# Sample retention in a decoder step: eight batch rows one at a time, or two at a time on 128 partitions

## The chip, the cores and the metric

The kernel is one program on one core of a Trainium2 chip. The metric is the device time of one launch in microseconds (us). The profile is of one execution of the program; it names the engines PE (TensorE), DVE (VectorE), ACT (ScalarE), POOL (GpSimd) and SP (the queue that issues the weight loads).

## The reference

The program is one layer of a hybrid decoder for 256 prompt tokens and 64 sample tokens (8 batch rows of 8 steps), all in float32. One input projection feeds three branches (window attention, retention, gated MLP), which are gated, summed and projected; then a mixture of 32 experts follows. The change is in the retention branch of the sample tokens, where every batch row has a state `S` of its own (8 heads, 64 x 128):

```python
def retention(q, k, v, s0):
    ...
    def step(S, xs):
        qc, kc, vc = xs
        a = jnp.einsum('bihd,bjhd->bhij', qc, kc) * intra
        o = jnp.einsum('bhij,bjhe->bihe', a, vc) + jnp.einsum('bihd,bhde->bihe', qc, S) * q_decay[None, :, :, None]
        S = S * c_decay[None, :, None, None] + jnp.einsum('bjhd,bjhe->bhde', kc * k_decay[None, :, :, None], vc)
        return S, o
...
    ob, s_new = retention(rq, rk, rv, s0)
    ob = head_norm(ob, ret_norm_g).astype(x.dtype) * jax.nn.silu(rg)
...
    x = x + g1 * ((ga * oa + gb * ob + gc * oc) @ w_out)
```

For the sample group a chunk is the 8 steps, so `step` runs once per batch row. Both `o` (8 tokens per batch row) and the new `S` (an output, 256 KB per batch row) are needed.

## The kernel before

There are five instruction streams, written by hand, that meet at semaphores. The order on each engine is the order of the code; nothing is scheduled by a planner.

**Weights.** SP streams units of 2 MB into three slots of `ring`; a slot is loaded again when PE has consumed its unit. The input projection has 19 units. A unit is three *pieces*, one for each token tile (128, 128 and 64 tokens), and `project(n)` on PE computes the next n pieces wherever it stands in the code: the small matmuls of the branches stand between pieces. The last units are RG0, RG1 (retention gate, SiLU) and GB0, GB1 (the branch's sigmoid gate); `project` of tiles 0 and 1 is line 1264 and of tile 2 line 1271. Two further units are the output projection. Slots 3 to 5 of `ring` hold branch data (`XQK`, `XV`, `XC`, `XG`) until the branches are merged, and then expert weights. ACT empties each piece from PSUM (`take_pieces`, line 548).

**Small results** go through three PSUM banks in turn, in the order of the list `AUX`. PE waits with `aux_free(name)` until the result three places before has been taken; whoever takes a result signals `used(name)`.

**Sample retention, before.** The scores within the chunk (`ra2`) and their product with V (`ro2`, kept with features on partitions in `ro_s`) are done for all 64 sample tokens together. Then the loop `for b in range(BATCH_S)` runs on PE, DVE, POOL and ACT alike, one batch row at a time, on 64 partitions:

- PE: the state's part of the output (`ri{b}`, line 1458), the update of the state in two halves (`rs2{b}{h}`, line 1467), then `SAMPLE_PIECES[b]` pieces of projection.
- DVE: adds `ri{b}` to `ro_s` (line 1001); adds each half of the update to the state and multiplies by the decay (lines 1007, 1010), into `V[0:64, 2]`. That buffer has one copy, so from the second batch row on DVE first waits until the row before has been stored (`state_stored`).
- POOL: loads the state of row b (two buffers, `V[0:64, b % 2]`), masks the keys to the batch row (`kd`, line 453), stores the state of the row before (line 456), and in between scales the SiLU gate (line 463) and adds the bias of GB0 and GB1 (line 417).

Between the rows DVE also runs `head_norm(t)` and `merge_gmlp(t)` for tiles 0 and 1; `head_norm` hands its squares to ACT (`square_heads`, line 655) and waits for them. After the loop PE turns `ro_s` back to tokens on partitions (`rback0`, `rback1`), DVE merges tiles 0 and 1 (`merge_retention`, lines 1024 and 1025), and then does `head_norm(2)` and the merge of tile 2.

**Behind it.** PE transposes the merged tiles (line 1200), spreads the gates `g1` (line 1223), runs the output projection, and the residual, router and expert loop follow. ACT may overwrite `V` with `g1` only when all states are stored. POOL loads and splits the experts' biases (lines 490 to 498) once all three tiles are merged.

## Time and profile before

| | us |
|---|---|
| median of 3 runs | 1681.4 |
| lowest and highest of the 3 | 1680.76 and 1681.45 |
| the profiled execution, from its first to its last instruction (span) | 1684.8 |
| of it: up to the first instruction of sample retention by batch row | 496.9 |
| the loop over batch rows, from there to the first transposes of merged tiles | 96.5 |
| from there to the first matmul of the expert loop | 93.0 |
| expert loop to the end | 998.4 |

The page gives the span as the time of the profiled execution and nothing around it. TensorE is busy in 94% of it, VectorE in 29%, ScalarE in 19%, GpSimd in 6%. The stretches are read off the starts of PE's instructions in the timeline (496.86, 593.44 and 686.42 us).

### The profile page before, as it was taken

Reading aid. Unit: us, or ns where it says so; the run is one execution under the profiler, and the core shown is the slowest. Engines: PE = TensorE matmul, PEld = TensorE weight load, DVE = VectorE, ACT = ScalarE, POOL = GpSimd, SP = SyncE. Lnnn points to the kernel's source line nnn. Section 1 sums busy time; section 2 is a strip of 40 time slices with the busy share of each in tenths; the row PEclk is TensorE's granted clock in tenths of the full one; section 3 lists DMA queues with packets and bytes.
Section 4 is the critical chain, followed back from the end, with each engine's and each line's share of the span. In section 5 each row is a group of like instructions: output and inputs, shape, how many; then the busy total and the mean of one; then the engine's idle time right before and its main releaser. Section 6 shows DMA issues by size and latency. Waiting matters only on the chain.

```text
span 1684.8 us, 20411 instructions
## 1 busy us (share of the span) xinstructions
PE 1590.9 (94%) x8125; PEld 696.9 (41%) x8126; DVE 489.1 (29%) x824; ACT 317.7 (19%) x582; POOL 105.6 (6%) x107
## 2 busy tenths in 40 slices
PE   4989898979999888899999999999999999999996
PEld 4455555444565656233333333333333333333332
DVE  2141222266024645322222222222122222222224
ACT  1123332112121133111111111111111111111120
POOL 0000000112113433000000000000000000000000
PEclk8989999989999888999999999999999999999999
DMA  9462532233223363599999999999593999999993
GB/s 361 170 253 100 204 146 85 103 110 106 94 85 131 103 218 113 221 418 429 429 428 428 429 428 429 429 429 428 244 419 155 417 424 429 428 429 429 428 428 140
DMA packets 38583, 491.89 MB, mean 292 GB/s; under 512 B 4784, under 2 KB 4912, under 8 KB 9744
## 3 DMA queue, kind: packets, MB, share of 16 engines
q1 hardware_dynamic: 34144, 477.27, 68.5%
q0 software_dynamic: 4400, 14.06, 2.9%
q8 instruction: 29, 0.48, 0.1%
q14 instruction: 10, 0.08, 0.0%
HBM read 486.99 MB, written 4.33 MB: 292 GB/s over the span
## 4 chain that ended last, share of the span: by engine, by line
PE 88%; DVE 4%; DMA 4%; ACT 2%; POOL 1%; issue 1%; SPq 0%; DVEq 0%; POOLq 0%
PE ps L1592 28%; PE ps L1264 17%; PE ps L1621 14%; PE ps L1555 6%; PE ps L1541 6%; PE ps L1200 4%; PE ps L1271 4%; DMA ring<-in_w_dense 2%; PE ps L1216 1%; PE ps L1223 1%; PE ps L1597 1%; DMA out_sample_retention<-V 1%; PE ps L1322 1%; PE ps L1342 1%; PE ps L1467 1%
## 5 line engine op out<-in xcount | busy, mean ns | idle before, releaser
L1592 PE MATMUL ps<-ring,arena 128*64 128x512 f32 x2176 | 480.2, 594 | 2.8 <-issue 2.8
L1264 PE MATMUL ps<-ring,xT 128*128 128x512 f32 x672 | 313.0, 624 | 2.9 <-DMA ring<-in_w_dense 2.1
L1592 PEld LDWEIGHTS ps<-ring,arena 128*64 128x64 f32 x2176 | 156.5, 137 | 308.3 <-issue 305.7
L1621 PE MATMUL ps<-ring,arena 128*64 128x512 f32 x1088 | 248.5, 599 | 0.0
L1264 PEld LDWEIGHTS ps<-ring,xT 128*128 128x128 f32 x672 | 131.4, 200 | 165.1 <-issue 160.8
L1178 DVE TENSOR_TENSOR U<-ps,U 128x1024 f32<-128x1024 f32 (+1 forms) x102 | 124.4, 1219 | 248.8 <-PE ps L1555 248.8
L1621 PEld LDWEIGHTS ps<-ring,arena 128*64 128x64 f32 x1088 | 72.0, 137 | 168.1 <-issue 142.3
L1555 PE MATMUL ps<-arena 64*128 64x512 f32 x420 | 119.6, 636 | 0.8 <-ACT arena L734 0.8
L1541 PE MATMUL ps<-T,arena 128*64 128x512 f32 (+1 forms) x420 | 104.4, 616 | 1.2 <-DVE arena L1068 1.2
L1169 DVE TENSOR_SCALAR arena<-ps 128x512 f32<-128x512 f32 x34 | 23.5, 692 | 217.4 <-PE ps L1597 217.4
L707 ACT ACTIVATE W<-ps 128x512 f32<-128x512 f32 x35 | 21.0, 599 | 338.5 <-PE ps L1541 338.5
L1167 DVE TENSOR_SCALAR arena<-ps 128x512 f32<-128x512 f32 x34 | 23.5, 691 | 188.0 <-PE ps L1597 188.0
L1271 PE MATMUL ps<-ring,xT 128*64 128x256 f32 x672 | 77.5, 384 | 0.0
L725 ACT ACTIVATE arena<-arena 128x512 f32<-128x512 f32 x34 | 21.4, 629 | 204.5 <-DVE arena L1167 204.5
L548 ACT ACTIVATE ring<-ps 128x512 f32<-128x512 f32 (+1 forms) x48 | 23.4, 488 | 191.4 <-PE ps L1264 159.4
L1271 PEld LDWEIGHTS ps<-ring,xT 128*64 128x64 f32 x672 | 46.6, 138 | 29.7 <-issue 7.9
L1541 PEld LDWEIGHTS ps<-T,arena 128*64 128x64 f32 (+1 forms) x420 | 24.2, 136 | 76.6 <-issue 76.6
L1200 PEld LDWEIGHTS ps<-consts,arena 128*128 128x128 f32 (+3 forms) x329 | 36.1, 138 | 42.3 <-issue 40.9
L731 ACT ACTIVATE arena<-ps 128x320 f32<-128x320 f32 x34 | 14.9, 437 | 203.3 <-PE ps L1555 203.3
L1200 PE MATMUL ps<-consts,arena 128*128 128x128 f32 (+3 forms) x329 | 50.0, 280 | 0.5 <-ACT arena L622 0.5
L1216 PE MATMUL ps<-ring 128*32 128x128 f32 x768 | 32.5, 342 | 18.1 <-DMA ring<-in_w_dense 18.1
L1555 PEld LDWEIGHTS ps<-arena 64*128 64x128 f32 x420 | 33.6, 190 | 29.6 <-issue 29.6
(258 smaller groups left out, 1122.9 us busy)
## 6 DMA issues: line engine op xcount, KB each, us to landing
ring<-in_w_moe SPq DMA_DIRECT2D x192, 2048.0 KB, 14.8
ring<-in_w_dense SPq DMA_DIRECT2D x33, 2048.0 KB, 8.8
V<-in_state POOLq DMA_DIRECT2D x8, 256.0 KB, 5.7
out_sample_retention<-V POOLq DMA_DIRECT2D x8, 256.0 KB, 3.1
R<-in_x_prompt SPq DMA_DIRECT2D x1, 1024.0 KB, 16.6
arena<-in_cache_kT POOLq DMA_DIRECT2D x8, 128.0 KB, 3.7
arena<-in_cache_v POOLq DMA_DIRECT2D x8, 128.0 KB, 3.7
arena<-in_b_gate POOLq DMA_DIRECT2D x4, 256.0 KB, 4.0
```

Source lines behind the costliest of these rows:

```text
L548: A(buf[0:ROWS[t], t, c0 + c:c0 + c + w], src, func).then_inc(z_used, 1)
L1167: X.tensor_scalar(g_cut, ps[:, 0, :], LIMIT, None, ALU.min).then_inc(g_cut_ready, 1)
L1169: X.tensor_scalar(u_cut, ps[:, 1, :], LIMIT, -LIMIT, ALU.min, ALU.max).then_inc(dve_step, 1)
L1178: X.tensor_tensor(both, ps[0:r, 6:8, :], both, ALU.add).then_inc(added, 1)
L1200: return nc.tensor.transpose(out, in_, ident[0:r, 0:r], **kw)
L1216: last = mm(aux_bank(name)[32 * j:32 * j + 32, 0:128], silu_c[:, k, :], wv[:, k, 128 * j:128 * j + 128], start=(k == 0), stop=(k == KD - 1 ...
L1264: last = mm(banks[t][0], xT[:, k, t * P:t * P + P], wv[:, k, :], start=(k == 0), stop=(k == KD - 1))
L1271: last = mm(banks[2 + a][0], xT[:, k, 2 * P:TOKENS], wv[:, k, 256 * a:256 * a + 256], start=(k == 0), stop=(k == KD - 1), skip_group_check ...
L1541: last = mm(ps[64 * a:64 * a + 64, 3, :], pick[0:r, t, :], T[0:r, t, HALF * a:HALF * a + HALF], start=(t == 0), stop=(t == 2), skip_group_ ...
L1555: last = mm(ps[:, first + a, :], gateT[64 * a:64 * a + 64, t * P:(t + 1) * P], y_blk[64 * a:64 * a + 64, :], start=True, stop=True)
L1592: last = mm(ps[64 * a:64 * a + 64, half, :], xgT[:, k, j % 2, :], wv[:, k, HALF * a:HALF * a + HALF], start=(j % 2 == 0 and k == 0), stop= ...
L1621: last = mm(ps[64 * a:64 * a + 64, 2, :], actT[:, k, j - 4, :], wv[:, k, HALF * a:HALF * a + HALF], start=(j == 4 and k == 0), stop=(j == ...
```

## The change

The batch rows are taken in four pairs. A pair's two states stand on the two halves of the 128 partitions. What changes:

- All states have a place of their own (`pair_state`: three in `V`, one in `XV`), are loaded ahead and updated in place.
- The transposed queries are copied to both halves (`rqT_s`) and multiplied with a mask of 0 and 1 (`q_batch`, a new input of 128 KB, loaded with the gMLP's parameters) into `q_of`: four copies, each with the tokens of one pair only.
- The state's part of the output is summed in PSUM over the four pairs on top of the score products, with tokens on partitions (`ro2`; heads alternate between PSUM partitions 0 to 63 and 64 to 127). `ri`, `ro_s` and the turning back `rback` are gone.
- The keys are masked twice instead of eight times (`k_of`), each to two batch rows side by side, and the update is a matmul over a group of 32 tokens that gives 128 partitions: `rs2{j}{h}{row}` is pair `j + 2 * row`, half h of the heads.
- DVE's order is now `head_norm(t)`, `merge_gmlp(t)`, `update_states(t)` for t = 0 and 1, then `head_norm(2)`, `merge_gmlp(2)`, the three `silu_times` and the three merges.
- `ret_gain` and `squares` move, and SP's loads of slots 3 to 5 also wait for the stores, since one pair stands in slot 3 to 5.

```diff
-for _b in range(BATCH_S):
-    AUX += [f"ri{_b}", f"rs2{_b}0", f"rs2{_b}1"]
-AUX += ["rback0", "rback1"]
+AUX += [f"rs2{j}{h}{r}" for j in range(2) for h in range(2) for r in range(2)]
...
-    kd = cut(4096, HALF)
-    ro_s = cut(4608, HALF)
-    ret_gain = XQK[:, 0, :]
-    squares = cut(1024, D)
+    rqT_s = cut(2560, RH, 64)
+    q_of = cut(0, 4, RH, 64)
+    q_batch = cut(5632, 4, 64)
+    k_of = XQK[0:64, 0:2, :].rearrange("p j (h b d) -> p j h b d", h=RH, b=2)
+    pair_state = [V[:, 0, :], V[:, 1, :], V[:, 2, :], XV[:, 0, :]]
+    ret_gain = cut(4096, D)
+    squares = XV[:, 1, :]
...
                 sp.wait_ge(merged, 3)
+                sp.wait_ge(state_stored, 16 * BATCH_S)
...
+        pool.dma_start(q_batch.rearrange("p n q -> p (n q)"), ins["q_batch"]).then_inc(gm_in, 16)
...
-        def load_state(b):
-            pool.dma_start(V[0:64, b % 2, :].rearrange("p (h e) -> p h e", h=RH),
-                           ins["state"][b].rearrange("h d e -> d h e")).then_inc(state_in[b % 2], 16)
+        def load_states(n):
+            for b in range(2):
+                pool.dma_start(pair_state[n][64 * b:64 * b + 64].rearrange("p (h e) -> p h e", h=RH),
+                               ins["state"][2 * n + b].rearrange("h d e -> d h e")).then_inc(state_in[n], 16)
+        def store_states(n):
+            for b in range(2):
+                pool.dma_start(outs["sample_retention"][2 * n + b].rearrange("h d e -> d h e"),
+                               pair_state[n][64 * b:64 * b + 64].rearrange("p (h e) -> p h e", h=RH)).then_inc(state_stored, 16)
         pool.wait_ge(gate_bias_in, 16)
         load_gate_bias(2, 0)
         pool.wait_ge(kv_stored, 64)
-        for b in range(2):
-            load_state(b)
-        pool.wait_ge(gm_in, 64)
+        for n in range(3):
+            load_states(n)
+        pool.wait_ge(gm_in, 80)
...
-        for b in range(BATCH_S):
-            if b >= 2:
-                pool.wait_ge(new_state, 2 * (b - 1))
-                load_state(b)
-            if b == 0:
-                pool.wait_ge(roped, 3)
...
-            nc.gpsimd.tensor_scalar(kd[0:64], XQK[0:64, 2, HALF:D], const("of_batch")[0:64, b:b + 1], None, ALU.mult).then_inc(kd_ready, 1)
-            if b >= 1:
-                pool.wait_ge(new_state, 2 * b)
-                pool.dma_start(outs["sample_retention"][b - 1].rearrange("h d e -> d h e"),
...
-                pool.wait_ge(z_used, 4 * (RG1 + 1))
-                pool.wait_ge(ret_gain_in, 16)
-                for t, r in enumerate(ROWS):
...
-            if b == 5:
-                add_gate_bias(XC, 0, GB0, 4)
-                load_gate_bias(1, 1)
...
-        pool.wait_ge(new_state, 2 * BATCH_S)
...
+        load_states(3)
+        pool.wait_ge(roped, 3)
+        k3 = XQK[0:64, 2, HALF:D].rearrange("p (h d) -> p h d", h=RH).unsqueeze(2).to_broadcast([64, RH, 2, RDK])
+        for j in range(2):
+            of = const("k_batch")[0:64, 2 * j:2 * j + 2].unsqueeze(1).unsqueeze(3).to_broadcast([64, RH, 2, RDK])
+            nc.gpsimd.tensor_tensor(k_of[:, j], k3, of, ALU.mult).then_inc(k_masked, 1)
+        pool.wait_ge(z_used, 4 * (RG1 + 1))
+        pool.wait_ge(ret_gain_in, 16)
+        for t, r in enumerate(ROWS):
+            nc.gpsimd.tensor_tensor(XG[0:r, t, :], XG[0:r, t, :], ret_gain[0:r], ALU.mult).then_inc(silu_scaled, 1)
+        pool.wait_ge(new_state, 4)
+        store_states(0)
+        store_states(2)
+        add_gate_bias(XC, 0, GB0, 4)
+        load_gate_bias(1, 1)
+        pool.wait_ge(new_state, 8)
+        store_states(1)
+        store_states(3)
+        add_gate_bias(XC, 1, GB1, 5)
         pool.dma_start(outs["prompt_retention"].rearrange("h d e -> d h e"), state[0:64]).then_inc(retention_stored, 16)
...
+        aux_filled(act, "rqT2")
+        turned_q = aux_bank("rqT2")[0:64].rearrange("p (h m) -> p h m", h=8)
+        A(rqT_s[0:64], turned_q, ACT.Copy)
+        A(rqT_s[64:128], turned_q, ACT.Copy).then_inc(used("rqT2"), 1)
+        aux_filled(act, "rkT2")
...
+        gate(R, 6, 1)
         aux_filled(act, "ro2")
-        A(ro_s, aux_bank("ro2"), ACT.Copy).then_inc(used("ro2"), 1)
-        gate(R, 6, 1)
+        by_parity = U[0:64, 2, :].rearrange("p (h a e) -> p a h e", h=4, a=2)
+        A(by_parity[:, 0], aux_bank("ro2")[0:64].rearrange("p (h e) -> p h e", h=4), ACT.Copy)
+        A(by_parity[:, 1], aux_bank("ro2")[64:128].rearrange("p (h e) -> p h e", h=4), ACT.Copy).then_inc(used("ro2"), 1)
...
-        for b in range(BATCH_S):
-            take_pieces(SAMPLE_PIECES[b])
-            if b in (1, 3):
-                square_heads(b // 2)
+        for t in range(3):
+            take_pieces(2)
+            square_heads(t)
+        take_pieces(2)
         gate(XC, 12, 1)
-        for h in range(2):
-            name = f"rback{h}"
-            aux_filled(act, name)
-            A(U[0:64, 2, HALF * h:HALF * h + HALF], aux_bank(name)[0:64], ACT.Copy).then_inc(used(name), 1)
-        square_heads(2)
...
+        aux_taken(dve, "rqT2")
+        X.tensor_tensor(q_of, rqT_s.unsqueeze(1).to_broadcast([P, 4, RH, 64]),
+                        q_batch.unsqueeze(2).to_broadcast([P, 4, RH, 64]), ALU.mult).then_inc(q_masked, 1)
...
+        def update_states(j):
+            for h in range(2):
+                for row in range(2):
+                    name = f"rs2{j}{h}{row}"
+                    aux_filled(dve, name)
+                    st = pair_state[j + 2 * row][:, HALF * h:HALF * h + HALF]
+                    X.tensor_tensor(st, aux_bank(name), st, ALU.add).then_inc(used(name), 1)
+                    aux_taken(dve, name)
+                    s4 = st.rearrange("p (h e) -> p h e", h=4)
+                    done(X.tensor_tensor(s4, s4, const("chunk_decay")[:, 8 + 4 * h:12 + 4 * h].unsqueeze(2).to_broadcast([P, 4, RDV]), ALU.mult), new_state)
+        aux_taken(dve, "ro00")
+        aux_taken(dve, "ro01")
+        head_norm(0)
+        merge_gmlp(0)
+        update_states(0)
+        aux_taken(dve, "ro10")
+        aux_taken(dve, "ro11")
+        head_norm(1)
+        merge_gmlp(1)
+        update_states(1)
         aux_taken(dve, "ro2")
-        for b in range(BATCH_S):
-            if b:
-                dve.wait_ge(state_stored, 16 * b)
-            name = f"ri{b}"
-            aux_filled(dve, name)
-            mine = ro_s.rearrange("p (h t) -> p h t", h=RH)[:, :, b * STEPS:(b + 1) * STEPS]
-            X.tensor_tensor(mine, aux_bank(name)[:, 0:64].rearrange("p (h t) -> p h t", h=RH), mine, ALU.add).then_inc(used(name), 1)
-            for h in range(2):
-                name = f"rs2{b}{h}"
-                aux_filled(dve, name)
-                st = V[0:64, b % 2, HALF * h:HALF * h + HALF]
-                new = V[0:64, 2, HALF * h:HALF * h + HALF]
-                X.tensor_tensor(new, aux_bank(name)[0:64], st, ALU.add).then_inc(used(name), 1)
-                aux_taken(dve, name)
-                n4 = new.rearrange("p (h e) -> p h e", h=4)
-                done(X.tensor_tensor(n4, n4, const("chunk_decay")[0:64, 8 + 4 * h:12 + 4 * h].unsqueeze(2).to_broadcast([64, 4, RDV]), ALU.mult), new_state)
-            if b in (1, 3):
-                aux_taken(dve, f"ro{b // 2}0")
-                aux_taken(dve, f"ro{b // 2}1")
-                head_norm(b // 2)
-            if b in (0, 2, 4):
-                merge_gmlp(b // 2)
-            if b in (5, 6):
-                silu_times(b - 5)
+        head_norm(2)
+        merge_gmlp(2)
+        for t in range(3):
+            silu_times(t)
...
-        merge_retention(0)
-        merge_retention(1)
-        aux_taken(dve, "rback0")
-        aux_taken(dve, "rback1")
-        head_norm(2)
-        silu_times(2)
-        merge_retention(2)
+        for t in range(3):
+            merge_retention(t)
...
+        def sample_out(n):
+            return aux_bank("ro2")[64 * (n % 2):64 * (n % 2) + 64, n // 2 * RDV:(n // 2 + 1) * RDV]
         for n in range(RH):
-            last = mm(aux_bank("ro2")[:, n * 64:n * 64 + 64], XV[0:64, 2, n * RDV:(n + 1) * RDV], ra[0:64, 0, n * 64:n * 64 + 64], start=True, stop=True)
+            mm(sample_out(n), ra[0:64, 0, n * 64:n * 64 + 64], XV[0:64, 2, n * RDV:(n + 1) * RDV], start=(n < 2), stop=False, skip_group_check=True)
+        pe.wait_ge(q_masked, 1)
+        for i in range(4):
+            pe.wait_ge(state_in[i], 32)
+            for n in range(RH):
+                last = mm(sample_out(n), q_of[:, i, n, :], pair_state[i][:, n * RDV:(n + 1) * RDV], start=False, stop=(i == 3), skip_group_check=True)
         last.then_inc(aux_ready, 1)
-        for b in range(BATCH_S):
-            pe.wait_ge(state_in[b % 2], 16 * (b // 2 + 1))
-            name = f"ri{b}"
-            aux_free(name)
-            for n in range(RH):
-                last = mm(aux_bank(name)[:, n * STEPS:(n + 1) * STEPS], V[0:64, b % 2, n * RDV:(n + 1) * RDV],
-                          rqT[0:64, n, b * STEPS:(b + 1) * STEPS], start=True, stop=True)
-            last.then_inc(aux_ready, 1)
-            pe.wait_ge(kd_ready, b + 1)
+        project(2)
+        for j in range(2):
+            pe.wait_ge(k_masked, j + 1)
             for h in range(2):
-                name = f"rs2{b}{h}"
-                aux_free(name)
+                names = [f"rs2{j}{h}{row}" for row in range(2)]
+                for name in names:
+                    aux_free(name)
                 for n in range(4):
                     hh = 4 * h + n
-                    last = mm(aux_bank(name)[0:64, n * P:n * P + P], kd[0:64, hh * RDK:(hh + 1) * RDK],
-                              XV[0:64, 2, hh * RDV:(hh + 1) * RDV], start=True, stop=True)
-                last.then_inc(aux_ready, 1)
-            project(SAMPLE_PIECES[b])
-        aux_taken(pe, f"ri{BATCH_S - 1}")
-        for h in range(2):
-            name = f"rback{h}"
-            aux_free(name)
-            for n in range(4):
-                hh = 4 * h + n
-                last = tr(aux_bank(name)[0:64, n * P:n * P + P], ro_s[:, hh * 64:hh * 64 + 64], P)
-            last.then_inc(aux_ready, 1)
+                    for row, name in enumerate(names):
+                        last = mm(aux_bank(name)[:, n * P:n * P + P], k_of[32 * row:32 * row + 32, j, hh].rearrange("p b d -> p (b d)"),
+                                  XV[32 * row:32 * row + 32, 2, hh * RDV:(hh + 1) * RDV], start=True, stop=True)
+                last.then_inc(aux_ready, 2)
+                project(1)
...
+def query_batches():
+    own = np.arange(64)[None, None, :] // STEPS == np.arange(BATCH_S).reshape(4, 2).T[:, :, None]
+    return np.repeat(own, 64, axis=0).reshape(P, -1).astype(np.float32)
```

On PE, from the score products of the sample (`ro2`) on; line 1264 is pieces of tiles 0 and 1 (x8 for one piece), line 1271 a piece of tile 2. Before:

```order
L1450 MATMUL ps<-arena,ring 128x64 x8
L1458 MATMUL ps<-arena,V 128x8 x8
L1467 MATMUL ps<-ring,arena 64x128 x8
L1264 MATMUL ps<-ring,xT 128x512 x8
L1271 MATMUL ps<-ring,xT 64x256 x16
L1458 MATMUL ps<-arena,V 128x8 x8
L1467 MATMUL ps<-ring,arena 64x128 x8
L1264 MATMUL ps<-ring,xT 128x512 x16
```

The same place after the change:

```order
L1457 MATMUL ps<-ring,arena 64x128 x8
L1462 MATMUL ps<-V,arena 64x128 x24
L1462 MATMUL ps<-ring,arena 64x128 x8
L1264 MATMUL ps<-ring,xT 128x512 x8
L1271 MATMUL ps<-ring,xT 64x256 x16
L1475 MATMUL ps<-ring 128x128 x8
L1264 MATMUL ps<-ring,xT 128x512 x8
L1475 MATMUL ps<-ring 128x128 x8
L1264 MATMUL ps<-ring,xT 128x512 x8
L1475 MATMUL ps<-ring 128x128 x8
L1271 MATMUL ps<-ring,xT 64x256 x16
L1475 MATMUL ps<-ring 128x128 x8
```

The state's matmuls now all stand in one place (line 1462), and of the update there are four groups (line 1475), each with one piece behind it; the eight pieces that were spread over eight batch rows follow with the last two together.

On DVE, from the masking of the sample's scores (line 963) on. Before, with the first batch row and `merge_gmlp(0)`:

```order
L963 TENSOR_TENSOR arena<-ps,consts 64x512
L1001 TENSOR_TENSOR arena<-ps,arena 128x8x8
L1007 TENSOR_TENSOR V<-ps,V 64x512
L1010 TENSOR_TENSOR V<-V,consts 64x512
L1007 TENSOR_TENSOR V<-ps,V 64x512
L1010 TENSOR_TENSOR V<-V,consts 64x512
L984 TENSOR_TENSOR W<-W,R 128x1024
L985 TENSOR_TENSOR T<-T,W 128x1024
```

The same place after the change, up to the first half state:

```order
L963 TENSOR_TENSOR arena<-ps,consts 64x512
L966 TENSOR_TENSOR arena<-arena 128x2048
L973 TENSOR_REDUCE stat<-U 128x8
L974 TENSOR_SCALAR stat<-stat 128x8
L975 TENSOR_TENSOR U<-U,stat 128x1024
L977 TENSOR_REDUCE stat<-ring 128x8
L978 TENSOR_SCALAR stat<-stat 128x8
L980 RECIPROCAL stat<-stat 128x8
L981 TENSOR_TENSOR U<-U,stat 128x1024
L987 TENSOR_TENSOR W<-W,R 128x1024
L988 TENSOR_TENSOR T<-T,W 128x1024
L1004 TENSOR_TENSOR V<-ps,V 128x512
```

`head_norm(0)` (lines 973 to 981) and `merge_gmlp(0)` (987, 988) now stand ahead of the first state update (1004), which frees PE's banks.

On ACT, in the residual behind the output projection, where the sum of squares (line 694) is followed by a square root (line 515); a piece of the difference:

```order
 L548 ACTIVATE W<-ps 128x512
 L694 ACTIVATE W,stat<-R 128x1024
+L515 ACT_TABLE_LOAD
 L515 ACTIVATE stat<-stat 128x1
 L548 ACTIVATE W<-ps 128x512
```

Before, the table of the square root was still loaded from `head_norm(2)`; now the sigmoid of the gates comes last ahead of the residual, and the load of the table stands behind the first sum of squares.

## Rows read from the trace of the kernel before

**Rows 1.** The page, its first line

```profile
span 1684.8 us, 20411 instructions
```

**Rows 2.** Chain that ended last, 495 to 605 us: start, us, what

```profile
562.69 4.78 POOL ring L417 x3
...
570.93 10.51 DMA out_sample_retention<-V
```

**Rows 3.** Timeline of DVE, the mask of the sample's scores

```profile
488.14 0.68 DVE L963 TENSOR_TENSOR arena<-ps,consts 64x512 f32<-64x512 f32 x1 [3.68 <-PE ps L1444]
```

**Rows 4.** Timeline of PE: start, us, what, [idle before it]

```profile
495.02 2.00 PE L1450 MATMUL ps<-arena,ring 64*128 64x64 f32 x16
...
501.64 9.40 PE L1264 MATMUL ps<-ring,xT 128*128 128x512 f32 x16
...
516.45 1.96 PE L1467 MATMUL ps<-ring,arena 64*64 64x128 f32 x16
...
518.34 14.00 PE L1264 MATMUL ps<-ring,xT 128*128 128x512 f32 x32
...
566.76 3.67 PE L1271 MATMUL ps<-ring,xT 128*64 128x256 f32 x32
...
575.57 3.67 PE L1467 MATMUL ps<-ring,arena 64*64 64x128 f32 x16
...
593.44 1.97 PE L1200 MATMUL ps<-consts,T 128*128 128x128 f32 x8 [2.37 <-DVE T L1025]
...
603.93 1.09 PE L1223 MATMUL ps<-mod,consts 128*64 128x128 f32 x8 [2.92 <-ACT V L675]
...
604.95 15.70 PE L1264 MATMUL ps<-ring,xT 128*128 128x512 f32 x32
```

**Rows 5.** Timeline of PE, other places

```profile
172.63 1.95 PE L1216 MATMUL ps<-ring 128*32 128x128 f32 x64
...
702.44 1.13 PE L1555 MATMUL ps<-arena 64*128 64x512 f32 x4
```

**Rows 6.** Timeline of POOL and DVE, 520 to 542 us

```profile
521.45 6.94 POOL L463 TENSOR_TENSOR ring<-ring 128x1024 f32<-128x1024 f32 x3
...
521.69 6.74 DVE L971 TENSOR_SCALAR stat<-stat 128x8 f32<-128x8 f32 x1
...
537.42 0.67 DVE L1007 TENSOR_TENSOR V<-ps,V 64x512 f32<-64x512 f32 x1
...
541.54 1.23 DVE L985 TENSOR_TENSOR T<-T,W 128x1024 f32<-128x1024 f32 x1
```

**Rows 7.** Chain and timeline around the gMLP's parameters, 357 to 373 us

```profile
357.39 8.46 DMA arena<-in_mixT_s
...
372.32 3.78 PE L1390 MATMUL ps<-ring,arena 128*128 128x128 f32 x16 [8.04 <-DVE ring L930]
```

**Rows 8.** Timeline of ACT, 570 to 646 us

```profile
570.48 0.78 ACT L548 ACTIVATE ring<-ps 64x256 f32<-64x256 f32 x2 [6.78 <-PE ps L1271]
...
573.21 1.06 ACT L554 ACTIVATE ring<-ring 128x1024 f32<-128x1024 f32 x1 [0.65 <-POOL ring L417]
...
599.71 1.28 ACT L515 ACT_TABLE_LOAD   x1
...
645.91 0.20 ACT L515 ACTIVATE stat<-stat 128x1 f32<-128x1 f32 x1 [0.29 <-DVE stat L760]
```

**Rows 9.** Timeline of POOL and DVE behind the merge

```profile
607.04 0.59 POOL L479 DMA_DIRECT2D arena<-in_router_w  x1 [12.68 <-DVE T L1025]
...
640.33 2.12 POOL L497 TENSOR_TENSOR U<-U,consts 32x1024 f32<-32x1024 f32 x1
...
640.43 2.56 DVE L1049 TENSOR_TENSOR W<-W,V 128x512 f32<-128x512 f32 x1 [5.47 <-ACT W L548]
```

**Rows 10.** Stretches: busy time of each engine, then granted clock of TensorE

```profile
512.00:533.00 21.00, 21.00 (x97) 11.77 (x93) 12.14 (x8) 1.98 (x5) 10.23 (x6) 1.00 0.37 125
...
580.00:593.00 13.00, 9.03 (x40) 8.00 (x40) 9.01 (x13) 1.18 (x2) 3.48 (x5) 0.50 0.16 38
```

43 lines of the change are left out of this document (18 added, 25 removed).

## The prediction

> **What bounds the kernel now.** The page gives a span of 1684.8 us [rows 1]; the median of the runs shown is 1681.4, 3.4 less. I make the sum against the span and move the median by it. First I read the chain that ended last between 495 and 605 us. Up to about 556 us it is PE alone. Then it hops: POOL's bias of the gates, a store of 10.51 us behind it, DVE, another store and DVE's merges [rows 2]. The single new-state buffer makes each batch row wait for the store of the row before. Next I read PE's timeline there: the last input piece ends at 566.76 + 3.67 = 570.43 us, the first transposes of merged tiles start at 593.44, and PE idles or works on crumbs at the lower clock between them (granted 0.50 in 580 to 593, which is 1.2 GHz, against 1.00, 2.4 GHz, in 512 to 533) [rows 4, 10]. So 23.0 us lie between last piece and merge, of which only the gate path is needed: ACT ends the first sigmoid at 573.21 + 1.06 = 574.27 us, 3.84 behind the last piece [rows 8]. Two DVE operations of 1.23 follow [rows 6]: 6.3 us would do. All behind it is PE's, in a row, up to the expert loop, whose loads are released by PE, so an earlier start moves the end by as much.
>
> **The change, part by part**, in times of the trace before (without what is added further up, which comes last).
>
> *PE, state outputs.* PE starts the score products at 495.02 [rows 4]. Now there are 8 + 32 small matmuls, 80 rows, since the profile counts a float32 matmul twice. They have 64 output partitions in alternating halves and 128 moving columns. From below: four column groups took 1.95 for 64, so two groups 0.061 each, 4.9 us [rows 5]. From above: the update's matmuls, all on one place, took 1.96 for 16, so 9.8 us; at the lower clock 3.67 for 16, so 18 us [rows 4]. The alternation makes it nearest to the column groups: I take 5.0, and PE is at the next piece at 500.0 (before: 501.64).
>
> *PE, pieces.* A piece of tile 0 or 1 takes 7.0 (14.00 for two), one of tile 2 takes 3.6, and the one at 501.64 took 9.40, as the clock was low behind the small matmuls [rows 4]. I keep the 9.40: RG1 ends at 500.0 + 9.4 + 3.6 = 513.0. The first update group (16 rows of 32 x 128) is priced like the old one, 1.96 [rows 4]: 515.0. GB0's first piece ends at 522.0. Of update groups there are four now, 7.8 us, where there were eight.
>
> A page of the Trainium skill (TensorEngine Tiling (Array Packing), Key Properties) says that different tiles of the array work in parallel, and that changing the tiling mode drains the engine. Trace: scatter matmuls in two row halves took 1.13 for 4 of 512 columns, less than the 0.44 each of a piece [rows 4, 5]. By that rule the four groups cost 1.0 each; the two that others wait for would bring 1.9 us more, 1656.5 in the end. I keep the row of the same size.
>
> *DVE.* The query mask is 2048 elements a partition; 1024 take 1.23 [rows 6], so 2.5 us, behind the mask of the scores (488.14 + 0.68 [rows 3]): 491.3. It is hidden: PE wants it behind the score products, at about 496. Then `head_norm(0)` centres tile 0 and waits for ACT's squares, which now stand behind RG1's last piece: 513.0, a copy of 0.78, a square of 1.06 (as a sigmoid of that size) [rows 8]: 514.9. POOL starts the SiLU scaling at the same moment, and it takes 6.94; in the trace a DVE TENSOR_SCALAR of 128x8 that met it took 6.74 [rows 6]. I expect the same here, at the variance: DVE stands until 520.9. Square root, reciprocal and multiply 2.1, `merge_gmlp` 2.5: at 525.5 the first half state is added (0.7, then 0.7 for the decay [rows 6]; the same on 128 partitions as on 64), and a bank is free at 526.2. **This is the new wait**: the second update group needs that bank, and all pieces are queued behind it on PE. It idles 522.0 to 526.2.
>
> Then the group 1.95, GB0's second piece 7.0, and 2.5 for the clock behind the wait (between 15.70 against 14.00 for two pieces, and 9.40 against 7.0 for one [rows 4]): 537.7. ACT takes it, squares tile 1: 539.4. DVE finishes `head_norm(1)` (3.2) and `merge_gmlp(1)` (2.5), adds: 545.8. PE meanwhile did the third group and GB0's last piece by 543.3, and waits 2.5 for that bank. Group 1.95, piece 7.0, clock 2.5: 557.3. Two more pieces: the last ends at 568.0 (before 570.43). DVE by then: updates to 552.4, centring to 555.0, squares of tile 2 at 559.0, `head_norm(2)` 562.2, merge 564.7, three SiLU products of 1.23: 568.4. The first gate is ready at 568.0 + 3.84 = 571.8, so DVE is not late, by 3.4 us. The merge is there at 574.3 against 593.44: **-19.1**.
>
> *Stores.* Eight stores and two late loads remain, but the loads are ahead of need and nothing on DVE waits for a store. ACT's wait before `g1` is for stores issued at about 553 to 555; even one of 10.51 us [rows 2] is down by 566.
>
> *ACT behind the merge.* Before, ACT was in tile 2's head norm, and PE waited 2.92 for it at 603.93 [rows 4]. That norm is now over: **-2.9**.
>
> *Table load.* The square root in the residual now loads its table. A load takes 1.28, and before ACT idled 0.29 there for DVE [rows 8]; DVE, ACT and PE all stand on that root: **+1.0**. The Trainium skill (ScalarE: Activation LUTs, What ACT_TABLE_LOAD costs) gives 1283 ns and a drain of 1380 ns. The load's row agrees, a drain is not a row of its own. By the page it would be +2.4, 1659.8 in the end.
>
> *POOL against DVE in the residual.* At 640.43 a DVE multiply of 512 elements, elsewhere 0.67, took 2.56, beside POOL's split of the expert bias [rows 6, 9]; the add behind it was late too, 0.7. POOL's split starts when all tiles are merged (607.04 [rows 9]). That now comes at 574.3 + 5.0 = 579.3, 28 earlier, while the residual moves by 22. The split (that part 33 to 35.4 behind its start, so 612.9 to 615) is over when the residual comes at 618.4: **-2.6**.
>
> *Further up.* `q_batch` is issued ahead of the gMLP's mixing weights. Their landing (8.46 after issue) is on the chain, and PE idles 8.04 for it [rows 7]. One more issue is 0.6 [rows 9]; 128 KB more at the rate of the 1.66 MB in those 8.46 is 0.65. From below 0, from above both, 1.2, and if the four further state loads behind it shared the queue, 5 more. I take **+0.6**.
>
> Sum: -19.1 - 2.9 + 1.0 - 2.6 + 0.6 = -23.0. Span 1661.8, median **1658.4**.
>
> **The rivals.**
> *Less is lost.* POOL doesn't meet DVE, banks are free in time, and the clock stays. Then PE could be through at 556, DVE at about 564: the merge comes 7.8 earlier still, 1650.6. For it: the stretch 512 to 533 held 1.00 with the same mix [rows 10]. Against it: the 6.74 row.
> *PE's new matmuls are dear.* 9.8 to 18 us in place of 5.0; squares, banks and pieces all move with them: 1663 to 1671. For it: the clock was low just there before [rows 4].
> *The parameters come late.* The state loads share the queue: +5, 1663. Against it: they are issued behind the awaited one.
> *Slower: the clock.* If the many small matmuls and the waits keep TensorE at 1.2 GHz through the pieces (five of 7.0 and three of 3.6, 46 us), these cost 46 more, of which 7.3 are counted: 1697. It decides once more than 23 + 7 = 30 of the 46 us run low. For it: 580 to 593 at 0.50. Against it: 512 to 533 at 1.00 with PE always busy.
> *It brings nothing.* Another wait holds the merge until 593, for instance a store. Against it: no reader waits for one. 1681.
>
> **How the numbers follow.** Forecast 0.50 (its own range 1653 to 1664), less lost 0.12, dear matmuls 0.20, late parameters 0.06, slower by the clock 0.04, nothing 0.03, and 0.05 for several costs at once, beyond 1672. The range takes the first four: 1650 to 1672. A measurement here tells about 0.2% (3.4 us) from no change. Faster by more 0.93, within 0.03, slower 0.04.
>
> **What would show it.** State outputs (line 1462) in about 5 us with the mask not waited for; DVE's TENSOR_SCALAR at the first variance as long as POOL's scaling; PE idle some 4 and 2.5 us ahead of the second and fourth group (line 1475), with DVE as releaser; last piece near 568, first transposes near 574 to 575; no wait for ACT ahead of the output projection; a table load behind the first sum of squares; the residual's first multiply of the second half back at 0.7. Wrong would be: no stall at the banks, DVE behind the gate, a low clock through whole pieces, or a wait on a state load or store.

## The result and the profile after

The changed kernel takes **1661.1 us** in the median of 4 runs (1652.7 to 1667.7), beside 1681.4 us before (1680.8 to 1683.7); the ratio is 0.986, 95% interval 0.983 to 0.989. Forecast was 1658.4, with a range of 1650 to 1672. The page of the profiled execution, first line:

```profile
span 1665.9 us, 20091 instructions
```

Against [rows 1] that is 18.9 us less, in one execution of each. The four executions of the changed kernel lie 15 us apart, so a difference of two spans says little by itself. What is compared below are stretches between fixed places of the program, each measured from where PE starts the sample's score products (`ro2`). First PE in the changed kernel (columns: start, us, engine, line, operation, output<-input, count, and in brackets the idle time before it with what ended it):

```profile
500.23 1.09 PE L1457 MATMUL ps<-ring,arena 64*64 64x128 f32 x16
501.25 2.84 PE L1462 MATMUL ps<-V,arena 128*64 128x128 f32 x48
...
504.89 7.13 PE L1264 MATMUL ps<-ring,xT 128*128 128x512 f32 x16
...
515.56 1.16 PE L1475 MATMUL ps<-ring 32*128 32x128 f32 x16
...
527.70 1.27 PE L1475 MATMUL ps<-ring 32*128 32x128 f32 x16 [3.91 <-DVE V L1004]
528.90 8.67 PE L1264 MATMUL ps<-ring,xT 128*128 128x512 f32 x16
...
546.82 2.08 PE L1475 MATMUL ps<-ring 32*128 32x128 f32 x16 [4.55 <-DVE V L1004]
548.83 15.81 PE L1264 MATMUL ps<-ring,xT 128*128 128x512 f32 x32
564.57 3.67 PE L1271 MATMUL ps<-ring,xT 128*64 128x256 f32 x32
575.33 1.97 PE L1200 MATMUL ps<-consts,T 128*128 128x128 f32 x8 [7.09 <-DVE T L1030]
...
583.48 14.00 PE L1264 MATMUL ps<-ring,xT 128*128 128x512 f32 x32
...
633.70 6.87 PE L1504 MATMUL ps<-arena,xT 128*128 128x32 f32 x32
```

L1457 are the score products with the values, L1462 the state outputs (64 rows in all; the first 48 are shown), L1475 the update groups, of which the third is left out. The reader should see four things. Score products and state outputs are over 4.66 us after their start, and the piece behind them takes 7.13, not the 9.40 of [rows 4]. PE waits for DVE before the second and the fourth update group, 3.91 and 4.55 us: the new wait that was forecast. Behind each wait PE is slower for a while (8.67 for a piece of 7.13; 2.08 for a group of 1.16). And there is no wait for ACT ahead of the output projection any more (583.48), where [rows 4] had 2.92.

DVE at the first head norm and the first half state:

```profile
518.76 0.17 DVE L978 TENSOR_SCALAR stat<-stat 128x8 f32<-128x8 f32 x1
...
519.52 2.77 DVE L981 TENSOR_TENSOR U<-U,stat 128x1024 f32<-128x1024 f32 x1
522.32 3.25 DVE L987 TENSOR_TENSOR W<-W,R 128x1024 f32<-128x1024 f32 x1
...
526.86 0.69 DVE L1004 TENSOR_TENSOR V<-ps,V 128x512 f32<-128x512 f32 x1
```

and POOL, which started its SiLU scaling a microsecond before DVE went on with the head norm (517.51):

```profile
516.54 7.95 POOL L462 TENSOR_TENSOR ring<-ring,arena 128x1024 f32<-128x1024 f32 x3 [22.99 <-ACT ring L548]
```

The TENSOR_SCALAR takes 0.17 us. In [rows 6] one beside the same scaling took 6.74, and the prediction had it stand until POOL was done. What is late instead are two TENSOR_TENSOR with two inputs each, 2.77 and 3.25 in place of 1.23.

The same stretches in all profiles, in us, each worked out from the starts of PE's groups (the last piece from start plus duration):

| kernel | score products start at | to the end of the last piece | to the first transposes | to the output projection | to the expert loop | score products to expert loop, sum |
|---|---|---|---|---|---|---|
| before | 495.0 | 75.4 | 23.0 | 11.5 | 81.5 | **191.4** |
| before_again | 489.9 | 75.4 | 23.3 | 11.5 | 81.4 | 191.7 |
| after | 500.2 | 68.0 | 7.1 | 8.2 | 83.1 | **166.4** |
| after_again | 492.8 | 67.9 | 7.1 | 8.1 | 83.1 | 166.2 |
| two_buffers | 489.4 | 75.4 | 20.4 | 12.0 | 80.0 | 187.9 |
| five_slots | 490.4 | 75.4 | 14.5 | 11.5 | 85.4 | 186.8 |
| no_alternating | 490.7 | 71.1 | 7.1 | 8.2 | 83.5 | 169.8 |
| scaling_by_tile | 490.3 | 61.7 | 7.1 | 7.9 | 80.7 | 157.4 |
| banks_first | 495.2 | 55.0 | 12.1 | 8.8 | 80.5 | 156.4 |
| table_early | 485.8 | 68.1 | 7.1 | 8.2 | 80.9 | 164.3 |
| residual_clean | 490.7 | 70.3 | 7.1 | 8.5 | 80.4 | 166.2 |
| combined | 503.4 | 55.0 | 10.6 | 7.7 | 80.3 | 153.6 |

The change takes 25.0 us out of the stretch that it touches (191.4 to 166.4; 25.5 between the two repeats). Up to the router's first products (line 1504 or its like) it is 161.6 us before and 133.5 after, 28.1 less. The first column moves by 17.6 us, among kernels that are the same up to there too; that is taken up at the end.

### The profile page after: what moved, and what is told of

It is laid out like the page before. It is cut to its first block, busy times and chain, and to the rows that moved or that the text cites. A ratio compares the mean times of both kernels' runs of the same rounds, so it can differ in the third digit from the quotient of the medians.

```text
span 1665.9 us, 20091 instructions
## 1 busy us (share of the span) xinstructions
PE 1566.5 (94%) x7989; PEld 670.2 (40%) x7990; DVE 483.0 (29%) x801; ACT 318.4 (19%) x582; POOL 97.6 (6%) x102
## 4 chain that ended last, share of the span: by engine, by line
PE 89%; DVE 4%; DMA 3%; ACT 2%; issue 1%; POOL 1%; SPq 0%; DVEq 0%; POOLq 0%
PE ps L1593 28%; PE ps L1264 17%; PE ps L1622 14%; PE ps L1542 6%; PE ps L1556 6%; PE ps L1271 5%; PE ps L1200 4%; DMA ring<-in_w_dense 2%; PE ps L1223 1%; PE ps L1216 1%; PE ps L1598 1%; PE ps L1322 1%; PE ps L1342 1%; ACT ring L548 1%; PE ps L1504 1%
## 5 line engine op out<-in xcount | busy, mean ns | idle before, releaser
L1264 PE MATMUL ps<-ring,xT 128*128 128x512 f32 x672 | 309.6, 618 | 3.0 <-DMA ring<-in_w_dense 2.3
L1271 PE MATMUL ps<-ring,xT 128*64 128x256 f32 x672 | 84.1, 407 | 0.0
L1200 PEld LDWEIGHTS ps<-consts,arena 128*128 128x128 f32 (+2 forms) x321 | 35.1, 138 | 41.9 <-issue 41.6
L1200 PE MATMUL ps<-consts,arena 128*128 128x128 f32 (+2 forms) x321 | 48.5, 278 | 0.5 <-ACT arena L622 0.5
L1216 PE MATMUL ps<-ring 128*32 128x128 f32 x768 | 28.3, 311 | 18.3 <-DMA ring<-in_w_dense 18.3
## 6 DMA issues: line engine op xcount, KB each, us to landing
R<-in_x_prompt SPq DMA_DIRECT2D x1, 1024.0 KB, 16.7
```

Of the source, the lines that this page charges most:

```text
L1200: return nc.tensor.transpose(out, in_, ident[0:r, 0:r], **kw)
L1216: last = mm(aux_bank(name)[32 * j:32 * j + 32, 0:128], silu_c[:, k, :], wv[:, k, 128 * j:128 * j + 128], start=(k == 0), stop=(k == KD - 1 ...
L1264: last = mm(banks[t][0], xT[:, k, t * P:t * P + P], wv[:, k, :], start=(k == 0), stop=(k == KD - 1))
L1271: last = mm(banks[2 + a][0], xT[:, k, 2 * P:TOKENS], wv[:, k, 256 * a:256 * a + 256], start=(k == 0), stop=(k == KD - 1), skip_group_check ...
```

## The experiments

Each kernel differs from one of the two by the lines shown and the semaphores that go with them. Times are medians, ratios are to the kernel before on the same chip (its medians there were 1683.8 to 1688.1), with their 95% interval; so go by the ratios across experiments.

### The two kernels again

> The changed kernel once more, nothing edited. Theory: its first profile drew about 5 us of low clock ahead of the change (PE reached the sample's score products at 500.23 us, before 495.02), so a second profile reaches them near 495 and has a span near 1660. Rival: the 5 us belong to the change (the new load of the query mask); then they are there again. Median of the runs 1656 to 1665 either way. From the score products to the expert loop 166.4 us (first profile) by both, plus or minus 2 for the clock.

**Measured:** 1657.4 us, ratio 0.985 (0.982 to 0.988).

> The kernel before once more, nothing edited: median 1681 within 3 us. Its profile shows how far two executions of one kernel lie apart in the part ahead of the score products (495.02 us in the first): 2 to 5 us if the clock's low stretches fall by chance, under 1 if they do not.

**Measured:** 1682.4 us, ratio 1.000 (0.997 to 1.003). The stretches of the table repeat within 0.4 us, the starts of the score products don't (495.0 and 489.9; 500.2 and 492.8). A span can't be compared within 1%. A stretch can be read to some tenths only where the clock falls alike: residual_clean, which is the changed kernel up to the last piece, takes 2.3 us longer there (70.3 for 68.0). A difference of two stretches is shown below only as far as single rows account for it.

### Only the row buffers: two_buffers, five_slots

In the kernel before, a batch row's new state goes into the one buffer `V[:, 2]`, and the next row waits for its store. First with two such buffers, everything else as before:

```diff
+    new_buf = [V[:, 2, :], XV[:, 0, :]]
...
-                dve.wait_ge(state_stored, 16 * b)
+                dve.wait_ge(row_stored[b % 2], 16 * (b // 2))
...
-                new = V[0:64, 2, HALF * h:HALF * h + HALF]
+                new = new_buf[b % 2][0:64, HALF * h:HALF * h + HALF]
```

> The kernel before, with two buffers for the new state instead of one, so that no batch row waits for the store of the row before it; everything else as before. Theory A (the chain of the last rows hangs on POOL, which issues the loads of states 6 and 7 between the gate biases, as much as on the store): DVE's waits for stores go, but PE still waits for the state of row 7, issued at about 576 us, and the time falls by 1 to 3 us only. Theory B (the single buffer was the bound): the 10.3 and 2.2 us that DVE waited for stores behind the last piece come off, 10 to 13 us less, more than half of what the whole change brought.

**Measured:** 1680.6 us, ratio 0.997 (0.996 to 0.999); the stretch is 3.5 us shorter, much nearer to theory A (1 to 3) than to B (10 to 13). The chain shows why not more; where the stores stood there is a load:

```profile
569.79 4.14 DMA V<-in_state
```

In the chain this load follows directly on POOL's gate bias (567.00 to 569.50 us), behind which it stands in POOL's program; besides, it may start only when the state two rows earlier has been used up. So, later, a second form with five slots, in which no load stands behind a gate bias:

```diff
+    slots = [V[:, 0, :], V[:, 1, :], V[:, 2, :], XV[:, 0, :], XV[:, 1, :]]
...
-                st = V[0:64, b % 2, HALF * h:HALF * h + HALF]
-                new = V[0:64, 2, HALF * h:HALF * h + HALF]
+                st = new = slots[b % 5][0:64, HALF * h:HALF * h + HALF]
```

> The kernel before, with one change: each batch row's state lives in one of five slots (V tiles 0 to 2, XV tiles 0 and 1), is updated in place and stored from there, and five rows are loaded ahead; rows 5 to 7 are loaded once the store of the row five before has landed, which was issued two rows earlier. All matmuls, masks and merges of the rows stay as they are, one row after the other. It asks how much of the 25 us between score products and expert loop comes from the row buffers alone. With two new-state buffers that stretch went from 191.4 to 187.9 us, and its chain still had 4.14 us of a state load and PE waits of 0.93 and 3.81 for loads. Theory A, buffers are a part, the work of the single rows (16 groups of products instead of 8, eight query groups, the sum carried back at the end) the rest: the load waits and the low clock behind them go, about 5 to 8 us: 180 to 183 us in that stretch, ratio to before 0.993 to 0.995. Theory B, the buffers are nearly all of it: 168 to 172 us, ratio 0.987 or less. Theory C, the rows now wait on DVE in place of the loads: 186 to 188, ratio 0.997 or more.

**Measured:** 1676.0 us, ratio 0.994 (0.991 to 0.996), the ratio of theory A, but the stretch, 186.8, is as theory C had it; the ratio holds the scatter ahead of the stretch too. The table tells where the gain went: the first transposes come 8.5 us sooner than before (14.5 against 23.0 behind the last piece), and 3.9 of these are lost again behind them. PE in the residual of this kernel:

```profile
569.53 3.14 PE L1463 MATMUL ps<-arena,V 64*128 64x8 f32 x16
572.60 3.67 PE L1472 MATMUL ps<-ring,arena 64*64 64x128 f32 x16
...
640.25 1.97 PE L1205 MATMUL ps<-consts,T 128*128 128x128 f32 x8 [4.86 <-ACT W L555]
...
644.18 6.88 PE L1508 MATMUL ps<-arena,xT 128*128 128x32 f32 x32
```

There is no wait for a state at 569.53 or 572.60, but the rows still come one after another on PE behind the last piece, at the lower clock (3.14 and 3.67 us; the row before had 1.95 and 1.96). At 640.25 PE waits 4.86 us, and the router products behind it take 6.88 where the kernel before needed 3.92 and two_buffers 4.08. So a merge that comes earlier can be worth less at the end than at the merge. The slow router products are in the changed kernel too (6.87 at 633.70), but an early merge alone doesn't bring them: scaling_by_tile and residual_clean, with merges as early, take 3.80 and 3.66. Why they fall on the lower clock in some kernels stays open.

Measured from the score products to the first transposes it is 98.4 us before, 89.9 with five slots and 75.1 in the changed kernel. Of 23.3 us, buffers bring **8.5**; the other **14.8** need the rest of the change: two rows on 128 partitions, no row left behind the last piece, the sum over rows made in PSUM, DVE's new order. No run parts these from each other. At the expert loop buffers are worth 4.6 of the 25.0.

### The order of the small matmuls: no_alternating

The state outputs go into alternating halves of the output, and the update groups take alternating 32-row groups of the array. Here the same matmuls run with equal halves and equal row groups one after the other:

```diff
+        HEADS = [0, 2, 4, 6, 1, 3, 5, 7]
-        for n in range(RH):
+        for n in HEADS:
             mm(sample_out(n), ra[0:64, 0, n * 64:n * 64 + 64], ...
...
-            for n in range(RH):
+            for n in HEADS:
                 last = mm(sample_out(n), q_of[:, i, n, :], ...
...
-                for n in range(4):
-                    hh = 4 * h + n
-                    for row, name in enumerate(names):
+                for row, name in enumerate(names):
+                    for n in range(4):
+                        hh = 4 * h + n
```

> The changed kernel with the heads of the state outputs in the order 0, 2, 4, 6, 1, 3, 5, 7 (all of one half of the PSUM partitions, then the other) and the update groups with all of one 32-row group, then the other; the same matmuls, other order. Theory (neighbours on different tiles of the array run at once): the state outputs take 9.4 to 9.8 us instead of 4.7, an update group 1.96 instead of 1.09; 5 to 8 us slower in all. Rival (a matmul of that size costs that little on its own): no difference, within 2 us.

**Measured:** 1660.0 us, ratio 0.986 (0.984 to 0.987); the stretch is 3.4 us longer than in after (3.7 than in after_again), which neither side had: 5 to 8 was the theory, under 2 the rival. PE's groups changed:

```profile
490.66 1.58 PE L1458 MATMUL ps<-ring,arena 64*64 64x128 f32 x16
...
507.30 1.71 PE L1476 MATMUL ps<-ring 32*128 32x128 f32 x16
...
519.44 3.06 PE L1476 MATMUL ps<-ring 32*128 32x128 f32 x16 [3.36 <-DVE V L1004]
```

A score group takes 1.58 in place of 1.09, an update group 1.71 in place of 1.16 at the higher clock, and 3.06 behind the waits (1.27 and 2.08 there). Score products and state outputs together take 5.97 for 4.66. So the order alone is worth a third of a group; neighbours on different parts of the array overlap. The first slower group is made up by a shorter wait behind it (3.36 for 3.91). The second wait is shorter by 1.5 (3.06 for 4.55): 0.55 by the slower third group, and 0.9 because DVE's last operation of `merge_gmlp(1)` doesn't meet POOL's gate bias here (1.23 us for the 2.17 in the changed kernel). The whole medians don't show the difference: 0.986 beside 0.986 and 0.985.

### The new wait: scaling_by_tile, banks_first

Two ways to take away PE's wait for a bank. In the first, POOL scales each tile of the SiLU as soon as ACT has it, rather than all three behind the last, beside DVE's head norm:

```diff
-        pool.wait_ge(z_used, 4 * (RG1 + 1))
         pool.wait_ge(ret_gain_in, 16)
         for t, r in enumerate(ROWS):
+            pool.wait_ge(z_used, 4 * RG1 + (1, 2, 4)[t])
```

> The changed kernel, with POOL's scaling of the SiLU gate waiting for each token tile of RG1 by itself instead of all three, so that two thirds of it run while DVE is idle. Theory (POOL's reads slow DVE's multiplies at the end of head_norm(0), 2.77 and 3.25 us in place of 1.23 each): they are back at 1.23, the first wait for a bank falls from 3.9 to about 0.4 us, and the kernel gains 3 to 5 us. Rival (those two are slow for another reason, or the wait is only moved to the second bank): within 1 us.

**Measured:** 1651.6 us, ratio 0.981 (0.977 to 0.985); the stretch is 9.0 us shorter, about twice what it had been put at. By the whole times alone the gain wouldn't be shown: the interval meets those of the changed kernel's two (0.982 to 0.989). DVE and PE:

```profile
509.60 1.23 DVE L981 TENSOR_TENSOR U<-U,stat 128x1024 f32<-128x1024 f32 x1
510.86 1.23 DVE L987 TENSOR_TENSOR W<-W,R 128x1024 f32<-128x1024 f32 x1
```

```profile
514.22 1.16 PE L1475 MATMUL ps<-ring 32*128 32x128 f32 x16 [0.35 <-DVE V L1004]
515.31 7.13 PE L1264 MATMUL ps<-ring,xT 128*128 128x512 f32 x16
...
531.69 1.55 PE L1475 MATMUL ps<-ring 32*128 32x128 f32 x16 [4.55 <-DVE V L1004]
...
617.69 3.80 PE L1504 MATMUL ps<-arena,xT 128*128 128x32 f32 x32
```

DVE's two operations are back at 1.23, and the first wait is 0.35 in place of 3.91 (-3.6). The group and the piece behind the vanished wait take 1.16 and 7.13 in place of 1.27 and 8.67 (-1.7). These 5.2 us the edit brought. The groups and pieces behind the second wait take 1.1 less, and 2.4 more are saved between output projection and expert loop, where the router products take 3.80 in place of 6.87; both are clock in places that nobody edited, and no run shows that the edit brought them. The second wait, 4.55, has not moved.

In the second way DVE hands over the banks of the first half earlier, while ACT squares the tile:

```diff
+            between()                      # in head_norm, behind the centring
             dve.wait_ge(head_squared, t + 1)
...
-        head_norm(0)
+        head_norm(0, lambda: update_states(0, (0,)))
         merge_gmlp(0)
-        update_states(0)
+        update_states(0, (1,))
```

> The changed kernel with DVE's order turned around at two places: the first half of the state update (heads 0 to 3) comes directly behind the centring in head_norm(0) and head_norm(1), where DVE waits for ACT's squares anyway, instead of behind head_norm and merge_gmlp. Theory (PE's 3.91 and 4.55 us of waiting for banks, and the clock behind them, set when the last piece ends): both waits go, the last piece ends 9 to 12 us earlier, and the kernel gains 5 to 10 us, less than the piece because DVE then has to catch up at the merge. Rival (DVE's own chain is the bound, PE's wait is only its shadow): 0 to 2 us.

**Measured:** 1649.0 us, ratio 0.979 (0.977 to 0.981), the stretch 10.0 us shorter; here the interval lies clear of the changed kernel's. PE, and DVE at the first merge:

```profile
518.72 1.16 PE L1476 MATMUL ps<-ring 32*128 32x128 f32 x16
519.81 7.13 PE L1265 MATMUL ps<-ring,xT 128*128 128x512 f32 x16
...
562.35 1.97 PE L1201 MATMUL ps<-consts,T 128*128 128x128 f32 x8 [12.09 <-DVE T L1031]
```

```profile
554.16 5.62 DVE L995 TENSOR_TENSOR U<-U,ring 128x1024 f32<-128x1024 f32 x3
559.81 1.23 DVE L1030 TENSOR_TENSOR U<-U,ring 128x1024 f32<-128x1024 f32 x1
```

No group waits for a bank, no piece is slow, and the last piece ends 13.0 us sooner. But the first transposes now stand 12.1 behind it and not 7.1: DVE has no idle time ahead of its first merge (559.81 follows on 554.16 + 5.62), so of 13 us 8 arrive. DVE, not PE, sets the merge now; its three SiLU products take 5.62 in place of 3.7, beside POOL's gate bias (551.25 to 557.45).

### The residual: residual_clean, table_early

Two costs behind the merge: the square root's table, and POOL's split of the expert bias beside DVE. The first kernel takes both away:

```diff
             pool.wait_ge(b1_in, 48 * (half + 1))
+            if half:
+                pool.wait_ge(h_ready, 3)
...
         gate(XC, 12, 1)
+        A(stat[:, 94:95], stat[:, 94:95], ACT.Sqrt)
```

> The changed kernel with a square root of an unused column put behind the gates on ACT, so that its table is loaded while PE transposes, and with the second half of POOL's split of the expert bias held back until the residual is over. Theory: DVE's wait for the square root in the residual falls from 1.36 to 0.34 us, the multiply and add of 1.66 and 1.41 go to 0.69 each, together 2.7 us less. Rival for the table (a load costs 2.7 us with a drain of its own): the first alone brings 2.4. Rival for the split: DVE is as slow as before, so POOL was not it.

**Measured:** 1658.2 us, ratio 0.983 (0.979 to 0.988). From output projection to expert loop 80.4 in place of 83.1 us; but 2.3 us more before it, where nothing was edited. DVE in the residual, of the changed kernel and then of this one:

```profile
617.27 1.66 DVE L1049 TENSOR_TENSOR W<-W,V 128x512 f32<-128x512 f32 x1 [3.08 <-ACT W L548]
618.97 1.41 DVE L1050 TENSOR_TENSOR R<-R,W 128x512 f32<-128x512 f32 x1
...
623.17 0.16 DVE L762 RECIPROCAL stat<-stat 128x1 f32<-128x1 f32 x1 [1.36 <-ACT stat L515]
```

```profile
610.33 0.69 DVE L1052 TENSOR_TENSOR W<-W,V 128x512 f32<-128x512 f32 x1 [5.47 <-ACT W L550]
611.06 0.69 DVE L1053 TENSOR_TENSOR R<-R,W 128x512 f32<-128x512 f32 x1
...
613.53 0.16 DVE L765 RECIPROCAL stat<-stat 128x1 f32<-128x1 f32 x1 [0.34 <-ACT stat L517]
```

Multiply and add fall from 1.66 and 1.41 to 0.69 each (-1.7 together), and the wait for the first root from 1.36 to 0.34 (-1.0). At the router's first products the edit has brought 2.6 us from the output projection on. That the expert loop shows the same 2.7 is luck: the router products take 3.66 and not 6.87, but POOL's held-back split now meets DVE's routing, and PE waits 3.79 us there in place of 1.98. Why the whole doesn't show the gain, PE tells:

```profile
518.15 1.68 PE L1478 MATMUL ps<-ring 32*128 32x128 f32 x16 [3.92 <-DVE V L1007]
519.76 9.94 PE L1267 MATMUL ps<-ring,xT 128*128 128x512 f32 x16
...
540.85 16.51 PE L1267 MATMUL ps<-ring,xT 128*128 128x512 f32 x32
```

The waits for the banks are those of the changed kernel, 3.92 and 4.55; what follows them is slower (1.68 for 1.27, 9.94 for 8.67, 16.51 for 15.81; 2.3 in all). That is the clock after the same waits, and not the edit: in combined, which has the edit and no such waits, that stretch is as short as in banks_first (55.0 both).

Then the table alone:

> The changed kernel with one square root of an unused column right behind the last sigmoid, so that its table is loaded while ACT has nothing to do; POOL's split is left where it is. If the table load costs what its row says and no more, DVE's wait for the first square root of the residual falls from 1.36 to 0.34 us, and the stretch from output projection to expert loop shrinks by 1.0 us where the clock is the same (83.1 to 82.1); DVE's multiply and add of the second half stay slowed by POOL (1.66 and 1.41 us). If a drain beyond the load was paid, it shrinks by 2.4.

**Measured:** 1650.2 us in one run. The wait for the root is 0.34:

```profile
607.76 0.16 DVE L763 RECIPROCAL stat<-stat 128x1 f32<-128x1 f32 x1 [0.34 <-ACT stat L515]
```

so the load costs 1.0, and multiply and add stay slow (1.62 and 1.41). The stretch to the expert loop is 80.9, 2.2 less than 83.1; 1.0 is the load, 1.1 are the products behind the router (line 1543) at a higher clock (4.46 for 5.58). The span is short above all because the score products started at 485.8.

### All of it: combined

The edits of scaling_by_tile, banks_first and residual_clean in one kernel.

> The changed kernel with the edits of three others together: first half of the state update ahead of the squares, scaling by tile, table and bias split out of the residual. If the terms add up: 5 to 10 plus 2.7 less than the changed kernel, scaling nearly nothing more since the bank wait is gone by then; median 1648 to 1654. If DVE's chain is the bound: 1656 to 1659.

**Measured:** 1646.7 us, ratio 0.977 (0.973 to 0.982), the lowest of all, though banks_first (0.977 to 0.981) can't be told from it; 0.8 to 0.9 points below the changed kernel's two. The stretch is 153.6 us, 12.8 less than in the changed kernel, about the sum of banks_first (10.0) and residual_clean's part behind the output projection (2.7); its profiled execution began it late, at 503.4. The chain that ended last goes through POOL here:

```profile
559.38 5.93 POOL ring L417 x3
```

The three additions of the gate's bias, 3.7 us in the changed kernel, take 5.9 beside DVE's three SiLU products, and these take 6.57 (559.81 to 566.38) in place of 3.7. The first merge follows them at 566.41 without idle time. It needs only the first tile's gate, which was there at 561.99, so it waited for DVE's own slowed products; the chain's hop to POOL comes from the third tile's gate, which happened to end in the same moment.

## Why the prediction was right

Direction, size and main mechanism held, and the nearness of the number is in part luck: two of the signs that had been named did not come (DVE's TENSOR_SCALAR held by POOL, the residual's multiply back at 0.7), and errors cancelled. The median is 2.7 us off the forecast, inside its own narrow range of 1653 to 1664, and the kernel's stretch from score products to expert loop was put at 167.8 us (191.4 - 19.1 - 2.9 + 1.0 - 2.6) and is 166.4. By its steps, distances from the start of the score products:

| step | predicted | after |
|---|---|---|
| next piece (state outputs done) | 5.0 | 4.66 |
| end of RG1 | 18.0 | 15.4 |
| second update group (first wait) | 31.2 | 27.5 |
| fourth update group (second wait) | 50.8 | 46.6 |
| last piece ends | 73.0 | 68.0 |
| first transposes | 79.3 | 75.1 |
| output projection | 87.9 | 83.3 |
| expert loop | 167.8 | 166.4 |

- **The store as what bound the kernel, half the reading.** The prediction named the single new-state buffer. Without it the merge moves by 2.6 us (98.4 to 95.8 from the score products), with no wait for loads either by 8.5; the other 14.8 of 23.3 are the rows themselves. The sum was not hurt, since it took the whole loop away.
- **State outputs, right in size.** 5.0 predicted, 4.66 measured; without the alternation 6.0 (496.63 less 490.66), so the upper bound of 9.8, taken from the old update's row, was no bound for this pattern. The rival of dear matmuls (9.8 to 18) is out.
- **RG1's first piece at 9.40, wrong.** It took 7.13: behind the new products the granted clock stays at 1.00, which is 2.4 GHz, from 500 to 520 us (the row stands at the end). That is 2.3 of the 5.0 us by which the last piece came sooner.
- **Update groups at 1.96, wrong in size.** They take 1.16 at the full clock. The prediction weighed against its row the rule of the Trainium skill (TensorEngine Tiling (Array Packing), Key Properties) that different tiles work in parallel, and put 1.0 on it. The runs side with that rule: 1.16 alternating, 1.71 without. Of the drain on a change of the tiling mode, which the same list states, no group shows anything. "The row of the same size" that I kept was one of matmuls all on one place.
- **DVE's TENSOR_SCALAR held by POOL, wrong; the wait behind it, right.** It took 0.17. I had carried over one row of 6.74 as if it belonged to the operation; beside the same scaling it did not recur. The collision fell on the two TENSOR_TENSOR instead, 3.6 us where I had DVE stand some 4.6, so the first wait came out at 3.91 for 4.2. scaling_by_tile shows cause and price: without POOL there, 0.35.
- **Second wait, 2.5 predicted, 4.55 measured.** PE was done 0.9 sooner behind GB0's second piece (group and small piece 4.7 for 5.6), and DVE handed over the bank 1.2 later behind it; 0.9 of that is one more meeting that I had left out, the second operation of `merge_gmlp(1)` at 543.77, 2.17 us in place of 1.23 beside POOL's gate bias (5.51 from 543.24). The updates behind it I had ending at 552.4, where 8 operations of 0.7 give 550.7; DVE was waiting for ACT's squares by then, so this had no effect.
- **Clock behind a wait, 2.5 each.** 1.5 behind the first, and 0.9 + 1.8 behind the second; in the four profiles with the same waits (after, after_again, table_early, residual_clean) the stretch to the last piece is 67.9 to 70.3.
- **Last piece to merge, 6.3 predicted, 7.09 measured.** The chain is the one named, copy, POOL's bias, ACT's sigmoid, two operations of DVE. The difference is a collision that I had left out:

```profile
569.22 1.27 POOL ring L417
...
570.51 1.06 ACT ring L554
...
571.67 2.36 DVE U L1029
```

  DVE's first product takes 2.36 beside POOL's next bias, not 1.23; the gate itself was ready 3.3 behind the last piece, not 3.84.
- **ACT's wait gone, -2.9 predicted, -3.4 measured.** From first transposes to output projection 11.5 before, 8.15 after.
- **Table load, +1.0, right.** 1.36 against 0.34 at the root, and table_early takes it away again. The Trainium skill (ScalarE: Activation LUTs, What ACT_TABLE_LOAD costs) would add a drain of 1380 ns; the trace doesn't agree, since load (1.28) and root together explain the wait.
- **POOL's split out of the way, -2.6, the step that failed.** I had this part end 3.4 us before the residual's multiply. It did not. POOL idled 14.75 us for the load of the bias, where it had been 12.62 before, and this part of the split came 35.7 behind POOL's first issue and not 33.3; and the residual came 2.4 sooner behind that issue than I had it, mostly because the output projection's first two pieces took 14.00 and no longer 15.70. So the split is still there:

```profile
597.42 1.03 POOL L493 CAST consts<-V 96x1024 bf16<-96x1024 f32 x1 [14.75 <-DMA V<-in_b]
...
616.26 2.12 POOL L497 TENSOR_TENSOR U<-U,consts 32x1024 f32<-32x1024 f32 x1
```

  at 617.27 DVE's multiply runs beside it. The two operations lose 1.7 in place of 2.6, so the change brought 0.9. Up to the router's first products the distance from the output projection is 1.4 less than before (50.2 for 51.7), nearly my -1.6. Then comes clock that I had nothing for: the router products take 6.87 for 3.92, of which 1.6 reach the end, since before PE waited 1.3 for DVE behind them, and the products and transposes behind the router (5.58 for 4.34, and two short groups) cost 1.8 more; between them 0.3 are won. From output projection to expert loop that makes +1.7 where I had -1.6. Whether the change brings this clock is open, as said at five_slots.
- **Transfer of `q_batch`, +0.6 predicted.** From POOL's first load there to the gMLP's products it is 16.7 us after and 16.5 before, so it costs 0.2; the landing in the chain takes 8.09, no longer than the 8.46 of [rows 7].

So the sum was right by errors that cancel in part: 4.2 us faster up to the merge, 0.5 more behind it, 3.3 worse in the residual and router. The profiled span, 1665.9 for 1661.8, is made of these -1.4, of 0.9 in the first expert group at the lower clock (9.72 us, 8.78 before), and of a start 5.2 later where 0.6 had been forecast. That start is scatter, not the change: after_again, the same kernel, starts at 492.8, and the eight of the changed form lie on both sides of the four of the old one (485.8 to 503.4, and 489.4 to 495.0).
